# Setup and input phases of an RWKV / differential-attention step merged into one start phase

## The reference

```python
def ada_mod(c, w, b, n):
    m = jnp.dot(jax.nn.silu(c), w) + b
    return jnp.split(m[:, None, :], n, axis=-1)
...
sh_m, sc_m, gt_m, sh_f, sc_f, gt_f = ada_mod(c, ada_w[l], ada_b[l], 6)
h = x * (1 + sc_m) + sh_m
...
# rwkv7_mix(h, prev, ...)
h_prev = jnp.concatenate([prev[:, None, :], h[:, :-1]], axis=1)
xx = h_prev - h
xs = h[None] + xx[None] * mu[:, None, None, :]
r, k, v = jnp.einsum('pbtd,pde->pbte', xs[:3], w_rkv)
```

## Time and profile before

| | |
|---|---|
| Time, median of 3 runs | 3733.06 us (3729.53 to 3743.84) |
| Span of the profiled execution | 3736.4 us, mean granted TensorE clock 0.933 |
| PE busy | 3337.8 us, 89% |
| DVE busy | 1968.1 us, 53% |
| ACT busy | 1443.2 us, 39% |
| POOL busy | 1754.5 us, 47% |
| DMA | 575.27 MB, mean 154 GB/s |

### The profile page before, as it was taken

One profiled execution on the slowest core, in us unless ns is written; L12 is line 12 of the kernel. 1 busy time (PEld: TensorE's weight loads), 2 busy tenths in 40 slices (PEclk: granted clock), 3 DMA queues, 4 the chain that ended last, 5 costly groups with the idle time before them and its releaser, 6 DMA issues. The chain is left out here.

```text
span 3736.4 us, 78971 instructions
## 1 busy us (share of the span) xinstructions
PE 3337.8 (89%) x34057; PEld 3074.3 (82%) x34057; DVE 1968.1 (53%) x2233; ACT 1443.2 (39%) x2361; POOL 1754.5 (47%) x716
## 2 busy tenths in 40 slices
PE   5999958999997199999999999877886999999997
PEld 2888857888886199999999999754555999999997
DVE  2976544555542664774333452098744747642432
ACT  1343423344332143443333343355564433433332
POOL 0666610000000166766666666465402666666664
PEclk8999978999997599999999999987888999999998
DMA  5555533433331544445445476567854444444442
GB/s 208 162 183 166 176 127 110 156 111 124 131 99 48 177 141 142 141 136 152 141 141 151 145 203 186 172 227 251 323 173 151 134 137 140 140 142 141 141 144 84
DMA packets 784518, 575.27 MB, mean 154 GB/s; under 512 B 45306, under 2 KB 747666, under 8 KB 783916
## 3 DMA queue, kind: packets, MB, share of 16 engines
q1 hardware_dynamic: 728806, 506.25, 44.3%
q10 hardware_dynamic: 55366, 63.98, 5.2%
HBM read 499.86 MB, written 70.29 MB: 153 GB/s over the span
## 5 line engine op out<-in xcount | busy, mean ns | idle before, releaser
L1662 POOL TENSOR_TENSOR dense_w_lo<-w_raw,dense_w_hi 128x1024 fp32r<-128x1024 f32 x504 | 1291.3, 2567 | 987.8 <-ACT dense_w_hi L1745 987.6
L1714 PE MATMUL acc<-dense_x_hi,dense_w_hi 128*128 128x344 f32 x2496 | 793.2, 322 | 27.2 <-DVE dense_x_lo L1851 20.9
L1715 PE MATMUL acc<-dense_x_lo,dense_w_hi 128*128 128x344 f32 x2496 | 788.6, 321 | 0.0
L1745 ACT ACTIVATE dense_w_hi<-w_raw 128x1024 fp32r<-128x1024 f32 x504 | 530.5, 1055 | 512.7 <-PE acc L1719 447.7
L1714 PEld LDWEIGHTS acc<-dense_x_hi,dense_w_hi 128*128 128x128 f32 x2496 | 470.9, 189 | 33.5 <-DVE dense_x_lo L1851 16.6
L1714 PE MATMUL acc<-dense_hid_hi,dense_w_hi 128*128 128x344 f32 x1536 | 487.2, 322 | 0.0
L1715 PE MATMUL acc<-dense_hid_lo,dense_w_hi 128*128 128x344 f32 x1536 | 483.4, 319 | 0.0
L1715 PEld LDWEIGHTS acc<-dense_x_lo,dense_w_hi 128*128 128x128 f32 x2496 | 471.2, 189 | 0.6
L1719 PE MATMUL acc<-dense_x_hi,dense_w_lo 128*128 128x344 f32 x2496 | 447.8, 322 | 2.2 <-POOL dense_w_lo L1662 2.2
L1719 PEld LDWEIGHTS acc<-dense_x_hi,dense_w_lo 128*128 128x128 f32 x2496 | 407.6, 189 | 2.7 <-POOL dense_w_lo L1662 2.7
L469 POOL TENSOR_TENSOR proj_w_lo<-proj_w_raw,proj_w_hi 128x1024 fp32r<-128x1024 f32 (+1 forms) x84 | 228.0, 2724 | 182.2 <-ACT proj_w_hi L564 182.0
(11 more groups left out here) (401 smaller groups left out, 6123.4 us busy)
## 6 DMA issues: line engine op xcount, KB each, us to landing
w_raw<-in_ffn_w SPq DMA_DIRECT2D x384, 512.0 KB, 4.2
ada_quarter<-in_ada_w SPq DMA_DIRECT2D x40, 1024.0 KB, 10.8
proj_w_raw<-in_a_w_rkv SPq DMA_DIRECT2D x72, 512.0 KB, 4.4
att_k_page<-in_cache_k SPq DMA_DIRECT2D x64, 512.0 KB, 4.2
att_v_page<-in_cache_v SPq DMA_DIRECT2D x64, 512.0 KB, 5.9
scratch_mix<-proj_stage ACTq DMA_DIRECT2D x72, 344.0 KB, 3.2
scratch_mix<-dense_stage ACTq DMA_DIRECT2D x72, 172.0 KB, 2.1
w_raw<-in_a_w_o SPq DMA_DIRECT2D x24, 512.0 KB, 4.5
```

The costliest lines, as they stand in the source:

```text
L1662: nc.gpsimd.tensor_tensor(wlo[:, i % NW], raw[:, i % NRAW], whi[:, i % NW].bitcast(F32), ALU.subtract).then_inc(S("lo"), 1)
L1714: T_.matmul(out, whi[:, s % NW, k, :], a, start=j.first and k == 0, stop=False)
L1715: T_.matmul(out, whi[:, s % NW, k, :], b, start=False, stop=False)
L1745: A(whi[:, i % NW], raw[:, i % NRAW], ACT.Copy).then_inc(S("hi"), 1)
```

## The change

`setup_phase` and `input_phase` become one `start_phase`, with one barrier less. SyncE loads the conditioning, sample and shift rows, then the four slabs, then the eight x row tiles; the 13 small vectors are loaded from ScalarE's queue. The conditioning rows are turned first and silu is formed on 128 x 72 columns. The ada products go to four column groups (eight matmuls per slab with 32 zero-padded weight columns, group k % 4), ScalarE copies 128 x 512, and a product with `fold`, four stacked identities, sums the groups and turns the rows at once. The slabs alternate between shift and scale, and the 1 is added with the bias. Each x row tile is then turned (eight blocks into one of three pairs of banks), copied into the full `x_cols` (128 x 8 x 1032) and modulated in eight VectorE instructions of 128 x 128. The scratch writes are issued after all eight tiles are copied, on a semaphore that outlives the phase; VectorE waits for it in `project_phase` before it first writes a buffer that may lie where `x_cols` was. The last rows of h are turned and sent out in `project_phase`, through ScalarE. The diff, with the removed lines mostly left out (they are those of the two functions above):

```diff
+        self.xt_out = ctx.enter_context(nc.semaphore("xt_out"))
...
-def setup_phase(m):
+def start_phase(m, h1, shT):
...
+        NU, NT = 4, KC
+        n9 = 1 + NS
+        x = sb("x_cols", [P, KC, T])
+        xin = sb("x_rows", [P, NT, D])
+        wide = sb("ada_slab", [P, NU, KC, 512])
+        crow = sb("c_rows", [n9, D])
+        xs, shin = sb("x_sample_rows", [NS, D]), sb("shift_rows", [NS, D])
         rows = sb("vec_rows", [P, 3, P])
...
+        def pair(t):
+            return six[:, 2 * (t % 3):2 * (t % 3) + 2, :]
+        def kind(u):
+            return u % 2, u // 2
         def ada_src(u):
-            mod, half = u // 2, u % 2
+            mod, half = kind(u)
             w = io["ada_w"][0, :, mod * D + half * 512:mod * D + half * 512 + 512]
             return w.rearrange("(k p) n -> p k n", p=P)
+        def halves(t, half):
+            return t[:, 4 * half:4 * half + 4]
         @block.sync
         def _(sp):
             nc.sync.dma_start(crow[0:1, :], io["c_prompt"]).then_inc(c_in, 16)
...
+            nc.sync.dma_start(crow[1:n9, :], io["c_sample"]).then_inc(c_in, 16)
+            nc.sync.dma_start(xs[:], io["x_sample"].rearrange("b o d -> (b o) d")).then_inc(s_in, 16)
+            nc.sync.dma_start(shin[:], io["state_shift"][0]).then_inc(s_in, 16)
+            for u in range(NU):
+                nc.sync.dma_start(wide[:, u], ada_src(u)).then_inc(landed[u], 16)
+            for t in range(NT):
+                nc.sync.dma_start(xin[:, t, :], io["x_prompt"][0, t * P:(t + 1) * P, :]).then_inc(x_in[t], 16)
+            sp.wait_ge(x_took, NT)
+            sp.wait_ge(smp_in, 2)
+            for c in range(KC):
+                nc.sync.dma_start(m.xt[c], x[:, c, :]).then_inc(m.xt_out, 16)
...
-                    nc.sync.dma_start(rows[at % P:at % P + q, at // P, :], flat[done:done + q, :]).then_inc(small, 16)
+                    nc.scalar.dma_start(rows[at % P:at % P + q, at // P, :], flat[done:done + q, :]).then_inc(small, 16)
...
+            act.wait_ge(ct_t, 1)
+            A(cexp[:], c_ps, ACT.Exp, scale=-1.0).then_inc(cexped, 1)
...
+                A(mrow[:, u % 2, :], m.aux[u % 2], ACT.Copy).then_inc(row_in, 1)
+            for t in range(NT):
+                act.wait_ge(x_t, t + 1)
+                A(x[:, :, t * P:(t + 1) * P], pair(t).rearrange("p b (c n) -> p (b c) n", n=P), ACT.Copy).then_inc(x_took, 1)
...
+            dve.wait_ge(ident1, 1)
+            for i in range(4):
+                gq = slice(32 * i, 32 * i + 32)
+                last = V.tensor_copy(fold[gq, :], m.ident[gq, 32 * i:32 * i + n9])
+            last.then_inc(folded, 1)
             dve.wait_ge(cexped, 1)
...
+            V.tensor_scalar_add(cden[:], cexp[:], 1.0).then_inc(csteps, 1)
             dve.wait_ge(csteps, 1)
...
+            V.reciprocal(cexp[:], cden[:]).then_inc(csteps, 1)
             dve.wait_ge(csteps, 2)
-            nc.vector.tensor_tensor(crow[:], crow[:], cexp[:], ALU.mult).then_inc(csteps, 1)
...
+            V.tensor_tensor(m.cT[:], c_ps, cexp[:], ALU.mult).then_inc(csteps, 1)
+            dve.wait_ge(csteps, 3)
+            dve.wait_ge(pads, 1)
+            V.tensor_copy(cpad[:, :, 0:n9], m.cT[:]).then_inc(cp_done, 1)
+            dve.wait_ge(xs_t, 1)
+            V.tensor_copy(x[:, :, SEQ:T], xs_ps).then_inc(smp_in, 1)
+            V.tensor_copy(shT[:], sh_ps).then_inc(smp_in, 1)
+            dve.wait_ge(vt_t, 1)
+            V.tensor_copy(m.vecs[:], m.aux[0][:, 0:NV * KC]).then_inc(vt_in, 1)
             dve.wait_ge(vt_in, 1)
+            dve.wait_ge(smp_in, 2)
             for u in range(NU):
...
+                mod, half = kind(u)
                 dve.wait_ge(mod_t, u + 1)
...
+                ps = six[:, u, 0:4 * n9].rearrange("p (k n) -> p k n", k=4)
+                bias = m.vecs[:, mod * KC + 4 * half:mod * KC + 4 * half + 4].unsqueeze(2).to_broadcast([P, 4, n9])
+                V.scalar_tensor_tensor(halves(m.mods[:, mod], half), ps, float(mod), bias, ALU.add, ALU.add).then_inc(mod_in, 1)
+                if mod == 0:
+                    continue
+                dve.wait_ge(mod_in, u + 1)
+                hs = halves(h, half)[:, :, SEQ:T]
+                V.tensor_tensor(hs, halves(x, half)[:, :, SEQ:T], halves(m.mods[:, M_SCM], half)[:, :, 1:], ALU.mult).then_inc(hs_done, 1)
+                dve.wait_ge(hs_done, half + 1)
+                V.tensor_tensor(hs, hs, halves(m.mods[:, M_SHM], half)[:, :, 1:], ALU.add)
             dve.wait_ge(mod_in, NU)
...
+            for t in range(NT):
+                dve.wait_ge(x_took, t + 1)
+                for c in range(KC):
+                    cols = slice(t * P, (t + 1) * P)
+                    V.tensor_scalar(h[:, c, cols], x[:, c, cols], m.mod(M_SCM, c), m.mod(M_SHM, c), ALU.mult, ALU.add)
...
+            pe.wait_ge(c_in, 32)
+            for k in range(KC):
+                last = T_.transpose(m.aux[1][:, k * n9:(k + 1) * n9], crow[:, k * P:(k + 1) * P], m.ident[0:n9, 0:n9])
+            last.then_inc(ct_t, 1)
+            pe.wait_ge(s_in, 32)
+            pe.wait_ge(csteps, 3)
+            for k in range(KC):
+                T_.transpose(m.aux[1][:, s0 + k * NS:s0 + (k + 1) * NS], xs[:, k * P:(k + 1) * P], m.ident[0:NS, 0:NS])
+                last = T_.transpose(m.aux[1][:, s1 + k * NS:s1 + (k + 1) * NS], shin[:, k * P:(k + 1) * P], m.ident[0:NS, 0:NS])
+            last.then_inc(xs_t, 1)
             pe.wait_ge(small, 16 * N_SMALL)
             left = NV * KC
             for t in range(3):
                 q = min(P, left - t * P)
...
+                last = T_.transpose(m.aux[0][:, t * P:t * P + q], rows[0:q, t, :], m.ident[0:q, 0:q])
+            last.then_inc(vt_t, 1)
+            pe.wait_ge(cp_done, 1)
+            pe.wait_ge(smp_in, 2)
+            pe.wait_ge(vt_in, 1)
+            pe.wait_ge(folded, 1)
             def turn(u):
                 pe.wait_ge(row_in, u + 1)
...
                 for q in range(4):
...
+                    last = T_.matmul(six[:, u, q * n9:(q + 1) * n9], mrow[:, u % 2, q * P:(q + 1) * P], fold[:], start=True, stop=True)
                 last.then_inc(mod_t, 1)
...
             for u in range(NU):
...
+                pe.wait_ge(landed[u], 16)
+                if u >= 2:
+                    pe.wait_ge(row_in, u - 1)
                 for k in range(KC):
-                    last = nc.tensor.matmul(m.acc[0][0:n, u % 3, :], cT[:, k, :], wide[:, u % NB, k, :],
-                                            start=(k == 0), stop=(k == KC - 1))
+                    gq = slice(32 * (k % 4), 32 * (k % 4) + 32)
+                    last = T_.matmul(m.aux[u % 2][gq, :], cpad[:, k, :], wide[:, u, k, :], start=(k < 4), stop=(k >= 4))
                 last.then_inc(ada_mm, 1)
...
+                turn(u)
+            for t in range(NT):
+                pe.wait_ge(x_in[t], 16)
+                if t == 0:
+                    pe.wait_ge(mod_in, NU)
+                if t >= 3:
+                    pe.wait_ge(x_took, t - 2)
+                for c in range(KC):
+                    last = T_.transpose(pair(t)[:, c // 4, (c % 4) * P:(c % 4 + 1) * P], xin[:, t, c * P:(c + 1) * P], m.ident[:])
+                last.then_inc(x_t, 1)
...
         GP = G - NS
+        late = [sb(f"x_{part}{x}", [P, KC, G], F32R) for x, part in ((1, "hi"), (1, "lo"), (2, "hi"))]
         raw = sb("w_raw", [P, NRAW, KC, P])
         whi, wlo = sb("w_hi", [P, NW, KC, P], F32R), sb("w_lo", [P, NW, KC, P], F32R)
-        xh, xl = sb("x_hi", [P, NX, KC, G], F32R), sb("x_lo", [P, NX, KC, G], F32R)
+        xh = [sb("x_hi0", [P, KC, G], F32R), late[0], late[2]]
+        xl = [sb("x_lo0", [P, KC, G], F32R), late[1], sb("x_lo2", [P, KC, G], F32R)]
...
+            n9 = 1 + NS
+            for c in range(KC):
+                last = T_.transpose(m.acc[1][0:n9, 1 + c // 4, (c % 4) * P:(c % 4 + 1) * P], h1[:, c, SEQ:1 + T], m.ident[:])
+            last.then_inc(S("rows_t"), 1)
             for i, j in enumerate(jobs):
+                if 4 in j.accs:
+                    need(pe, "rows_in", 1)
                 for a in j.accs:
...
+                        if use == 1:
+                            dve.wait_ge(m.xt_out, 16 * KC)
...
+            need(act, "rows_t", 1)
+            A(lastrows[:].rearrange("p (a n) -> p a n", a=2), m.acc[1][0:1 + NS, 1:3, :], ACT.Copy).then_inc(S("rows_in"), 1)
+            need(act, "rows_in", 1)
+            nc.scalar.dma_start(io["shift_prompt"][0], lastrows[0:1, :]).then_inc(S("rows_out"), 16)
+            nc.scalar.dma_start(io["shift_sample"][0], lastrows[1:1 + NS, :]).then_inc(S("rows_out"), 16)
...
+            need(act, "rows_out", 32)
...
-        setup_phase(m)
-        m.end_phase()
         with ExitStack() as mix:
             h = mix.enter_context(nc.sbuf_tensor("h", [P, KC, 1 + T], F32))
             shift = mix.enter_context(nc.sbuf_tensor("shift_cols", [P, KC, NS], F32))
-            input_phase(m, h, shift)
+            start_phase(m, h, shift)
             m.end_phase()
```

(34 more changed lines are left out.)

152 lines of the change are left out of this document (30 added, 122 removed).

## The result

The changed kernel takes 3705.03 us (median of 8 runs, 3700.55 to 3715.95) against 3733.06 (8 runs, 3717.35 to 3750.52) before: ratio 0.9927, 95% interval 0.9904 to 0.995, that is 27 us less with an interval of 19 to 36. The profiled execution has a span of 3710.5 us, 25.9 less than before.

The account below looks back on a forecast made before the run. The opening was taken as a row of stages up to 84.6 us, each with another limit; T0 36.6 us earlier, plus 0.6 for open ends, gave 36 us less, 3697 (band 3693 to 3702, range 3685 to 3711).

Parts of the forecast that it names:

- Loads: Start of the kernel: slab 0 issued at about 2.15 us instead of 6.53, last x tile landed at about 37.
- Small vectors: 13 loads on ScalarE's queue: ScalarE free at about 6.6 us, cT at 9.5, ada products starting at 13.0.
- Ada products: Four column groups: a slab's 16 instructions take 1.92 us at full clock, 3.8 at half; modulation columns complete at 31.5.
- The rival of the slower side: Column groups not side by side at half clock, 16.5 us per slab: 12 us more, 3745; chance 0.03.
- x tiles: Turning, copying and modulating x: 1.3 us modulation per tile, eighth copy at 42 to 43 us, VectorE done at about 45.
- T0: Start of the projection's first VectorE instruction (L527): forecast 48 us against 84.64 before, 36.6 us earlier.
- The scratch writes: SyncE's eight writes after the copies: 4.5 us of issue, bounds 2.6 to 5.5; SyncE last at the barrier, about 47.
- Barrier: Between the start phase and the projection phase: 0.8 us.
- Projection opening: First projection slab: weights land at T0 + 11, slab ends at T0 + 23.6; effect 0, bounds -4 to +3.
- for the open ends: An allowance of +0.6 us in the forecast's sum, beside the -36.6 us.
- the half-clock rival: TensorE stays at half clock, columns at 39.4, T0 56: 28.5 us less, 3704.5; chance 0.20 together with slow transposes.
- The rival that does nothing: The shorter opening's time returns as waiting in the first projection slabs; nothing or within 0.5%, chance 0.05.

Follow-up runs that it names:

- One_group: Changed kernel with the ada products in one column group, as before the change; one profiled run: columns at 47.5, T0 67.3, span 3715.7 us.
- Pairs: Changed kernel with x modulated two row tiles at a time, 32 VectorE instructions of 128x256 instead of 64 of 128x128; T0 51.24, profiled span 3692.7 us.
- both: Changed kernel with modulation by pairs of tiles and scratch writes issued behind the first four weight slabs; ratio to the kernel before 0.9895 (0.9871 to 0.992).
- writes_later: Changed kernel with the eight scratch writes issued in the projection phase, behind its first four weight slabs; T0 51.5, profiled span 3699.0 us.
- both_low_late: Kernel "both" with GpSimd waiting for the eight pieces of the first use before its first low part; first slab T0 + 20.0, profiled span 3706.1 us.
- after_again: The changed kernel once more, without edit; ratio to the kernel before 0.992 (0.9894 to 0.9947), T0 54.1.
- best: Changed kernel with pairs of tiles, writes behind four weight slabs, GpSimd's low parts after the eight pieces, and TensorE filler matmuls; ratio to before 0.9913 (0.9891 to 0.9935).
- low_late_timed: The same kernel as both_low_late, run again and timed; ratio to the kernel before 0.9919 (0.9902 to 0.9936).
- both_fill: Kernel "both" with filler matmuls on TensorE during its waits for silu(c) and around the slabs; T0 45.6, profiled span 3712.9 us.
- before_groups: Kernel before the change with the four column groups and fold alone; T0 75.0, profiled span 3726.6 us.

## Why the prediction was right, and where it was off

The median fell to 3705, inside the range of 3685 to 3711, and the side was right; the forecast of 3697 was 8 us too low. It lies outside the forecast's own band (3693 to 3702), and the wide range is part of why it held.

*Loads.* Slabs from 2.15, last tile before 37: right; the stream ends at about 35 (25 GB/s from 35.0 us on), with 413 GB/s where I took 387. The Trainium skill, "DMA: Bandwidth & Descriptors", section "Specifications", has about 358 GB/s as a core's HBM limit; the changed kernel's trace disagrees more clearly than the one before did.

*Small vectors.* ScalarE free at 6.3 (6.6 said), cT at 9.0 (9.5), first products at 12.51 (13.0): right.

*Ada products.* 1.92 and 3.6 us for a slab, as the attention row and its double said; 3.64, then two at 1.92, then the last at half clock. Columns at 32.3 (31.5). One_group prices the groups at 15.2 us. The rival of the slower side, groups that do not run side by side at half clock, is refuted by the 3.60 of the last slab, which needed over 13.5 to come true.

*x tiles.* The eighth copy at 42.5 (42 to 43): right. The modulation behind it is **the step that was mis-sized**. I took 1.3 us for a tile of eight instructions, from L338 and L339 starting 0.08 us apart, and gave 2.0, 0.25 for each instruction, as the bound if nothing overlaps. A tile took 16.50 / 8 = 2.06 us, 0.258 for each instruction: VectorE was done at 51.2, not 45. The reason given for the bound was wrong as well (durations min/median/max in ns, first and last start in us):

```profile
L270 DVE TENSOR_SCALAR h<-x_cols,mods x64: 338/341/349, 34.7 to 50.8; 128x128 f32<-128x128 f32 x64
```

Each instruction lasts 0.341 us and starts 0.258 behind the one before, so they do overlap, by 0.08 us, about as L338 (0.171 long) and L339 do. The 0.08 us from the start of a copy of 8 columns to the next start is not the fixed cost of an instruction in a row: even four copies of 9 columns in a row (the fold, 0.71 us in all, 0.168 each) start about 0.18 apart. The instructions of 256 columns last 0.407 and start 10.43 / 32 = 0.326 apart; with the 0.806 of 1024 columns the three durations lie on one line of 0.52 ns per column. From these I estimate a start distance of about 0.19 us plus 0.52 ns per column. Pairs shows it, and "both" with T0 47.6 gives back what the forecast (48) had promised.

*The scratch writes.* 7.87 us of issue, 4.5 taken, outside the bound of 5.5. The eight x loads that I went by took 5.46 us. This is the second mis-sized term, and the forecast's sum ran over it: SyncE was to reach the barrier last, at 47. Here it was hidden by the modulation, by 0.8 us; alone it would have put T0 at 51.2 (pairs).

*Barrier.* VectorE's end 51.18 to T0 52.1: 0.9, said 0.8.

*Projection opening.* T0 + 23.9, said T0 + 23.6. The weights came at T0 + 6.3, not T0 + 11, since T0 came later and the writes not; it made no difference, and writes_later made none either. Keeping GpSimd back until the eight pieces are done takes 3.8 us off it (both_low_late), and 3.4 to 3.6 come back as a wait for the second use.

So 32.5 us were saved instead of 36.6: 4.1 for the two mis-sized terms. The +0.6 "for the open ends" in the sum has no row behind it, and no run shows it. From 32.5 to the 27 measured (interval 19 to 36) nothing needs a cause: the interval holds 32.5, after_again gives 30 (20 to 40), and the table shows how the program behind T0 scatters. Over the timed kernels it is less clean: at T0, "both", "best" and low_late_timed are 37.0, 38.9 and 37.4 us earlier than before and measured 39, 32 and 30 less, the last with an interval of 24 to 37. That a few microseconds of an earlier start are lost again behind it is not excluded.

*The rivals.* The measured 3705 is the very time that the half-clock rival gave (3704.5), but that is chance and not its mechanism: its columns would have come at 39.4, and they came at 32.3. Half clock took its share (3.60 for 1.92, 8.85 for 7.18), 2.0 us of T0 by both_fill. Transposes do raise the clock and hold it. In the changed kernel only the 64 transposes ran on TensorE from 33.5 to 41.3 us, without a pause, and the granted clock (third number from the end) was 0.53 and then 0.90:

```profile
33.50:36.00 2.50, 2.50 (x15) 2.50 (x13) 1.32 (x6) 2.02 (x2) 0.00 (x0) 0.53 0.54 220
36.00:41.30 5.30, 5.29 (x44) 5.05 (x42) 5.30 (x22) 4.53 (x6) 0.00 (x0) 0.90 0.01 2
```

In both_fill 64 of them took 7.18 us at granted clock 1.00. By the Trainium skill, "TensorE: Matmul & The Clock Gate", section "Part 4: PE-mode transpose", such work does not count as busy for the clock gate; this trace disagrees as that of before did. The rival that does nothing is refuted as far as it goes: the time did not come back in the first projection slab (T0 + 23.9).

## What to carry to other kernels

Where an instruction is cut into many small ones, price the row of small ones by the fixed part of each (eight of 128 columns took 2.06 us here, one of 1024 took 0.81), not by the start distance of one unlike pair; the row can become the last thing at a barrier. When two engines reach a barrier within a microsecond of each other, neither edit alone shows its worth: 0.9 and 0.6 us alone, 4.5 together. And compare phases, not spans: a saving of 30 us at the front was plain to about 2 us at T0 (52.1 and 54.1 in two profiles of one kernel), while the 3650 us behind it scattered with a standard deviation of 7 us.

## What the runs showed of the hardware that I had not expected

- Issuing the scratch writes from SyncE cost far more in a row than alone: 0.32 us each when they came singly (L287 before), 7.87 us for eight back to back (7.86 to 7.90 in five executions), 0.33 for the first and 1.18 in the median, after the loads had run dry. It is not so for every row of DMAs: eight x loads of 512 KB took 3.76 us in before_groups and 5.46 in the kernel before, 0.44 and 0.43 in the median.
- A row of 128x128 tensor_scalar instructions between SBUF tiles starts one every 0.258 us, though each lasts 0.341 (16.49 to 16.50 us for 64 in five executions).
- Filler products of 4.6 us, with pauses of 0.56 and 0.70 us behind them, did not leave TensorE at full clock for the first slab (3.46 us in both_fill, 3.64 in best), while with fillers between the later slabs these took 1.92 us each.
- With the same 17416 TensorE instructions the scan phase took 725 to 747 us in fourteen executions, and TensorE's busy time in it 609 to 627, at granted clocks of 0.87 to 0.91. The longest has the lowest clock, but the order is not strict (0.91 at 730.4 us).
